# Layer norms of a second transformer block, with their sums made inside the product ahead of them

## The reference

```python
def _layer_norm(x, g, b, eps):
    mu = jnp.mean(xf, axis=-1, keepdims=True)
    var = jnp.mean(jnp.square(xf - mu), axis=-1, keepdims=True)
    return (xf - mu) * lax.rsqrt(var + eps) * g + b
...
for l in range(2):                       # ALPHA = 4 ** 0.25
    h = rwkv7_time_mix(x) if l == 0 else diff_attention(x, k_sh, v_sh)  # both end in @ w_o
    x = _layer_norm(ALPHA * x + h, ln_g[l, 0], ln_b[l, 0], 1e-5)
    x = _layer_norm(ALPHA * x + jnp.square(jax.nn.relu(x @ w1[l])) @ w2[l],
                    ln_g[l, 1], ln_b[l, 1], 1e-5)
```

## Time and profile before

| | us |
|---|---|
| median of 3 runs | 3045.97 (3044.67 to 3046.77) |
| the profiled execution's time | 3043.37 |
| its span | 3041.6 |
| PE busy | 2741.9 (90% of the span) |
| DVE, ACT, POOL busy | 1189.7, 517.5, 531.2 |
| mean granted TensorE clock | 0.928 of full speed |

### The profile page before, as it was taken

How to read it: one execution, slowest core, us unless ns; L and a number is a source line. 1 busy time by engine, 2 the same in 40 slices (tenths; PEclk the granted TensorE clock), 3 DMA queues, 4 the chain that set the end, 5 groups by cost and what they waited for, 6 DMA issues and landing times. The chain is left out here.

```text
span 3041.6 us, 45357 instructions
## 1 busy us (share of the span) xinstructions
PE 2741.9 (90%) x20202; PEld 2017.3 (66%) x20202; DVE 1189.7 (39%) x1791; ACT 517.5 (17%) x983; POOL 531.2 (17%) x304
## 2 busy tenths in 40 slices
PE   6999888977899997997888788999989998899997
PEld 4556577753688885443766646888854454688886
DVE  2221233443699944103565524442120062444312
ACT  3222112220211101013443301000010062100001
POOL 0000244520000000000222103344400000343331
PEclk9999867998899998998887888999989999899998
DMA  6222100020222123111000001222213100122220
GB/s 267 111 111 87 53 2 2 2 84 28 74 93 83 59 77 114 55 69 56 3 2 2 3 28 56 87 102 89 83 57 111 59 25 28 56 83 83 84 83 28
DMA packets 16210, 196.29 MB, mean 65 GB/s; under 512 B 1768, under 2 KB 1896, under 8 KB 4112
## 3 DMA queue, kind: packets, MB, share of 16 engines
q1 hardware_dynamic: 16016, 193.39, 16.8%
HBM read 191.27 MB, written 2.12 MB: 64 GB/s over the span
## 5 line engine op out<-in xcount | busy, mean ns | idle before, releaser
L2807 PE MATMUL psum<-arena,weight_ring 128*128 128x256 f32 x3072 | 674.6, 381 | 14.0 <-PEq L1607 14.0
L2807 PEld LDWEIGHTS psum<-arena,weight_ring 128*128 128x128 f32 x3072 | 587.7, 191 | 95.5 <-issue 14.5
L226 PE MATMUL psum<-arena,weight_ring 128*128 128x512 f32 x1024 | 450.7, 602 | 52.3 <-PEq L1474 26.1
L226 PEld LDWEIGHTS psum<-arena,weight_ring 128*128 128x128 f32 x1024 | 197.5, 194 | 302.2 <-issue 285.7
L1754 PE MATMUL psum<-arena,weight_ring 128*128 128x256 f32 x1584 | 349.3, 382 | 11.1 <-PEq L1607 7.0
L1754 PEld LDWEIGHTS psum<-arena,weight_ring 128*128 128x128 f32 x1584 | 303.5, 192 | 53.7 <-issue 11.7
L468 PE MATMUL psum<-arena,weight_ring 128*128 128x512 f32 (+1 forms) x672 | 248.2, 529 | 2.7 <-ACT arena L601 2.7
L2181 POOL TENSOR_TENSOR arena<-arena,consts_sb 128x512 f32<-128x512 f32 x48 | 64.5, 1350 | 1003.5 <-ACT arena L2473 775.4
L468 PEld LDWEIGHTS psum<-arena,weight_ring 128*128 128x128 f32 x672 | 128.2, 193 | 114.5 <-issue 106.4
L2855 POOL TENSOR_TENSOR arena<-weight_ring 128x1024 f32<-128x1024 f32 x32 | 77.0, 2407 | 548.5 <-issue 519.9
L2863 POOL TENSOR_TENSOR weight_ring<-arena,weight_ring 128x1024 f32<-128x1024 f32 x32 | 80.9, 2529 | 372.4 <-PE psum L2807 372.2
(11 more groups left out here) (410 smaller groups left out, 3397.9 us busy)
## 6 DMA issues: line engine op xcount, KB each, us to landing
weight_ring<-in_mlp_up SPq DMA_DIRECT2D x16, 2048.0 KB, 7.7
weight_ring<-in_mlp_down SPq DMA_DIRECT2D x16, 2048.0 KB, 7.7
weight_ring<-in_ada SPq DMA_DIRECT2D x12, 2048.0 KB, 13.0
weight_ring<-in_gate_up SPq DMA_DIRECT2D x11, 2048.0 KB, 7.6
weight_ring<-in_w_in SPq DMA_DIRECT2D x7, 2048.0 KB, 11.1
weight_ring<-in_w_o SPq DMA_DIRECT2D x4, 2048.0 KB, 7.8
weight_ring<-in_w_kv SPq DMA_DIRECT2D x4, 2048.0 KB, 8.0
weight_ring<-in_down_a SPq DMA_DIRECT2D x4, 1536.0 KB, 6.4
```

Source lines behind the costliest of these rows:

```text
L226: mm = pe.matmul(bank[:, 0:width], w[:, k, m * P:(m + 1) * P], rhs(k), start=(k == 0), stop=(k == kt - 1))
L2807: mm = pe.matmul(g.banks[i][:, pair * HALF:(pair + 1) * HALF], left[:, j, pair * P:(pair + 1) * P], right(j), start=first and j == 0, stop ...
```

## The change

The four `feature_norm` stages of the second block and `stage_store` are gone. Each norm's work is divided over the stage ahead of it and the stage behind it.

In the product ahead (`residual_product`, `mlp`): after the first output tile the token mean over that one tile's 128 features (a "shift") is made and subtracted from all tiles. Later tiles are scaled by ALPHA and shifted ahead of time, so that the eviction is a plain addition of the bank. VectorE keeps a running sum of the shifted tiles (`total`) and of their squares (`power`, the squares from ScalarE), and TensorE sums over the partitions only `total`, `power` and the last tile with its square. `tail_stats` then makes the mean, its square and that minus eps. In `mlp` the unit is not a tile but a part of 256 columns, 16 parts in four rounds; the TensorE work stands between products of chunks 10 and 15.

In the stage behind (`mlp`, `stage_qkv`, and a new `stage_last_norm`), the "head": variance, root, reciprocal, the two spreads, and then subtraction, multiplication and gain and bias tile by tile, each tile's `normed` counted. The stage's first products wait tile by tile: `mlp` does products 0, 2, 1, 3, ... of chunk 0 in that order, and makes each side as soon as its tiles are there; `stage_qkv` runs the first three key tiles in one loop over k. `stage_last_norm` writes each tile by a DMA of its own.

```diff
-def residual_product(g, chunks, kt, cols, src):
...
+def tile_sums(pe, g, bank, rows, quarters, first, last):
+    for i, j in enumerate(quarters):
+        mm = pe.matmul(bank[32 * j:32 * j + 32, 0:P], g.c.ones[:, 0:32], rows[:, i * P:(i + 1) * P],
+                       start=first, stop=last, skip_group_check=True)
+def tail_stats(g, dve, s):
+    dve.wait_ge(s.sums, 1)
+    dve.tensor_scalar(mean, g.banks[1][:, 0:P], 1.0 / D, None, ALU.mult).then_inc(s.stats, 1)
+    dve.wait_ge(s.stats, 1)
+    dve.tensor_tensor(square, mean, mean, ALU.mult).then_inc(s.stats, 1)
+    dve.wait_ge(s.stats, 2)
+    dve.tensor_scalar(square, square, -LN_EPS, None, ALU.add).then_inc(s.stats, 1)
...
+def residual_product(g, src):          # TensorE
+                    if m == 1:
+                        pe.wait_ge(g.acc_free, group0 + 1)
+                        tile_sums(pe, g, g.banks[7], x[:, 0, :], quarters, True, True).then_inc(s.first_sum, 1)
+                    if m == 2:
+                        pe.wait_ge(s.first_mean, 1)
+                        quarter_spread(pe, g, g.banks[5], first).then_inc(s.shift_all, 1)
+                pe.wait_ge(s.total, KD - 2)
+                tile_sums(pe, g, g.banks[1], total, quarters, True, False)
+                pe.wait_ge(s.power, KD - 2)
+                tile_sums(pe, g, g.banks[7], power, quarters, True, False)
+                tile_ready(pe, KD - 1)
+                tile_sums(pe, g, g.banks[1], x[:, KD - 1, :], quarters, False, True).then_inc(s.sums, 1)
+                pe.wait_ge(s.sq, KD)
+                tile_sums(pe, g, g.banks[7], sq[:, 1, :], quarters, False, True)
...
+def head_tiles(g, dve, s, lo, hi):
+    for k in range(lo, hi + 1):
+        if k == 0:
+            dve.wait_ge(s.mean_all, 1)
+        if k < hi or k == lo:
+            dve.tensor_tensor(x[:, k, :], x[:, k, :], g.banks[5][:, :], ALU.subtract).then_inc(s.centred, 1)
+        if k > lo:
+            dve.wait_ge(s.inv_all, 1)
+            dve.wait_ge(s.centred, k)
+            dve.tensor_tensor(x[:, k - 1, :], x[:, k - 1, :], g.banks[6][:, :], ALU.mult).then_inc(s.scaled, 1)
...
-def mlp(g):
+def mlp(g, norm):
+                            if c == 0 and pair == 0 and i < 2:
+                                pe.wait_ge(s.normed, 4 * i + j + 1)
...
+                def shift_work(c, i):
+                    if (c, i) == (UP + 2, 1):
+                        part_added(3)
+                        tile_sums(pe, g, g.banks[7], x[:, 0, :], range(4), True, True).then_inc(s.first_sum, 1)
+                    if (c, i) == (UP + 2, 4):
+                        pe.wait_ge(s.first_mean, 1)
+                        quarter_spread(pe, g, g.banks[7], first).then_inc(s.shift_all, 1)
+                    if (c, i) == (UP + 7, 5):
+                        pe.wait_ge(s.took, 6 * (UP + 3) + 1)
+                        pe.wait_ge(s.total, 10)
+                        pe.wait_ge(s.power, 10)
+                        for h in (0, 1):
+                            tile_sums(pe, g, g.banks[1], total[h], (2 * h, 2 * h + 1), True, False)
+                            tile_sums(pe, g, g.banks[7], power[h], (2 * h, 2 * h + 1), True, False)
+                        last_sums(12)
+                    if (c, i) == (UP + 7, 6):
+                        for n in (13, 14, 15):
+                            last_sums(n)
...
                     product(c, 0, a11, b11)
-                    product(c, 1, a12, b21)
+                    if c > 0:
+                        product(c, 1, a12, b21)
...
                     product(c, 2, s1, r1)
+                    if c == 0:
+                        product(c, 1, a12, b21)
...
+                first_product(UP + 5, UP + 2, HALF)          # ScalarE, down part
+                for n in range(4, 8):
+                    square(n)
+                first_product(UP + 7, UP + 3, HALF)
+                for n in range(8, 16):
+                    square(n)
...
+                head_inverse(g, dve, s)                      # VectorE, start of mlp
+                head_tiles(g, dve, s, 0, 5)
+                dve.wait_ge(s.normed, 4)
                 dve.tensor_tensor(up_t[0], x12, x11, ALU.subtract).then_inc(s.side, 1)
+                head_tiles(g, dve, s, 5, 8)
+                dve.wait_ge(s.normed, 8)
                 dve.tensor_tensor(up_t[2], x22, x12, ALU.subtract).then_inc(s.side, 1)
...
+                        if c < ALL - 1:                      # VectorE, after down_others of a round
+                            scale_and_shift((c - UP) // 2 + 1)
+                            add_up((c - UP) // 2)
...
-            sp.dma_start(g.out, x[:, :, :]).then_inc(g.stored, 16)
+                for k in range(KD):
+                    sp.wait_ge(s.normed, k + 1)
+                    sp.dma_start(g.out[:, k, :], x[:, k, :]).then_inc(g.stored, 16)
```

More of the change, by code:

```diff
@@ L2728, in _ @@
                 dve.wait_ge(s.out, KD)
[L2731 to L2743 removed]
+NORM_STAT_AT, SQUARE_AT, SHIFT_AT, FIRST_AT, TOTAL_AT = 12288, 12800, 13824, 14336, 14464
@@ new lines, with head_pe, head_act @@
+HEAD_SEMS = ("var", "root", "inv", "mean_all", "inv_all", "centred", "scaled", "normed")
+def head_pe(g, pe, s):
+    mean, _, inv = norm_stats(g)
+    quarter_spread(pe, g, g.banks[5], mean).then_inc(s.mean_all, 1)
+    pe.wait_ge(s.inv, 1)
+    quarter_spread(pe, g, g.banks[6], inv).then_inc(s.inv_all, 1)
+def head_act(g, act, s, n):
+    x, inv = view(g, X_AT, KD, SEQ), norm_stats(g)[2]
+    act.wait_ge(s.var, 1)
+    act.activation(inv, inv, ACT.Sqrt).then_inc(s.root, 1)
+    for k in range(KD):
+        act.wait_ge(s.scaled, k + 1)
+        act.activation(x[:, k, :], x[:, k, :], ACT.Identity, bias=g.v.ln_b[:, 8 * n + k:8 * n + k + 1],
+                       scale=g.v.ln_g[:, 8 * n + k:8 * n + k + 1]).then_inc(s.normed, 1)
@@ L2768, in mlp @@
     UP, ALL = 8, 16
+    sq = [view(g, at + HALF, HALF) for at in (MLP_V_AT, 35328 - HALF)] + [g.c.lvl[:, SEQ:SEQ + HALF], view(g, MLP_S1_AT, HALF)]
+    first = view(g, 35584, P)
+    shift = [view(g, at + HALF, HALF) for at in (MLP_P1_AT, MLP_U2_AT)]
+    parts = [(t, h) for m in range(4) for t, h in ((m, 0), (m + 4, 1), (m + 4, 0), (m, 1))]
+    down0 = group0 + KF2
+    total, power = ([at[:, HALF * h:HALF * h + HALF] for h in (0, 1)] for at in (g.c.lvl, g.c.scan))
     def quads(c):
@@ L2785, in mlp, with part_ready, part @@
     with ExitStack() as ctx:
-        s = stage_sems(g, ctx, "sums", "side", "side4", "prod", "p1", "took", "hid", "added")
+        s = stage_sems(g, ctx, "w_sums", "side", "side4", "prod", "p1", "took", "hid", "order", "added", "first_sum", "first_mean",
+                       "shift_all", "shift", "shifted", "sq", "total", "power", "sums", "stats", *HEAD_SEMS)
+        def part_ready(eng, n):
+            if n < 4:
+                eng.wait_ge(s.shifted, n + 1)
+            elif n % 4 == 3:
+                eng.wait_ge(g.acc_free, down0 + 2 * (n // 4) + 2)
+            else:
+                eng.wait_ge(s.added, 3 * (n // 4) + n % 4 + 1)
+        def part(n):
+            t, h = parts[n]
+            return x[:, t, HALF * h:HALF * h + HALF]
         with nc.Block() as block:
@@ L2801, in product @@
                             pe.wait_ge(g.acc_free, free_groups(r))
+                        elif i == 5 and r > UP:
+                            pe.wait_ge(s.added, 3 * (r - UP))
                         else:
@@ new lines, in down_others, with take_shift @@
+                    dve.tensor_tensor(x[:, m, hi], x[:, m, hi], g.banks[6][:, lo], ALU.add).then_inc(g.acc_free, 2)
+                def take_shift():
+                    dve.wait_ge(s.first_sum, 1)
+                    dve.tensor_scalar(first, g.banks[7][:, 0:P], 1.0 / P, None, ALU.mult).then_inc(s.first_mean, 1)
+                    dve.wait_ge(s.shift, 2)
+                    dve.wait_ge(s.added, 3)
+                    dve.wait_ge(g.acc_free, down0 + 2)
+                    for n in range(4):
+                        dve.tensor_tensor(part(n), part(n), shift[parts[n][1]], ALU.subtract).then_inc(s.shifted, 1)
```

274 lines of the change are left out of this document (221 added, 53 removed).

## The result

The changed kernel takes 2995.36 us (median of 4 runs, 2991.83 to 2999.48), the kernel before 3045.66 (4 runs). The ratio is 0.9835, 95% interval 0.9818 to 0.9852: 50 us less, where 47.6 were forecast (2998, range 2989 to 3008). The profiled execution took 2991.83, its span is 2990.0, the granted clock 0.939 on the mean.

The account below looks back on a forecast made before the run. TensorE is busy nine tenths of the span, so only its latency holes at the four norms can give: 23.8 + 13.6 + 10.2 = 47.6 off 3043.4 makes 2995.8, plus 2.6 for a median, rounded to 2998, range 2989 to 3008.

Parts of the forecast that it names:

- The chain of the head: Norm 0, counted from T, the last product's end: head at T + 2.65, product 0 at T + 7.1, tile 3 ready at 10.65.
- Norms 0 and 2: Norm and chunk 0 end at T + 36.7 instead of 49.7, less 1.1 in the product ahead: 11.9 us each.
- the hole: TensorE's gap at norm 0, from the last product of one stage to the first of the next: 22.4 us.
- the clock: Chunk 0 behind norms 0 and 2: the low TensorE clock was taken to cost 3.1 us.
- Norm 1: Norm and four key tiles end at T + 36.0 instead of 51.7, less 2.1 in `mlp`: 13.6 us saved.
- Norm 3: Last norm to the end: 16.8 instead of 29.1, less 2.1 for the down part: 10.2 us saved.
- A: Heads: the low clock lasts longer, a second 6 us stretch costing each of three heads 3: 3007; chance 0.12.
- worst form: All of chunk 0 and the first keys run at 1.2 GHz, 67 us more: 3065; chance 0.02.
- B: Last round of `mlp`: VectorE is late with its sums, TensorE stands 4 to 6 us in each: 3008; chance 0.08.
- C: Heads: the tile-by-tile start fails, the first product runs only once the eighth tile is normed: 3020; chance 0.03.
- D: Heads: the clock does not fall at all behind T, the last product's end: 2990.5; chance 0.05.

Follow-up runs that it names:

- no_shift: Changed kernel with the shift left out, evictions scaling and adding as before the change: 2991.76 us, ratio 0.9822.
- no_shift_fill: Changed kernel without the shift and with six matmuls of constants in the head of `mlp`: 2987.98 us, ratio 0.9807.
- fill: Changed kernel with six matmuls of constants put into the head of `mlp`: 2994.29 us, ratio 0.9826.
- all_normed: Changed kernel with the first product of each `mlp` and the first key matmul waiting for all eight tiles: 3017.76 us, ratio 0.9915.
- subs_first: Changed kernel with all eight subtractions of the head ahead of all multiplications: 3008.88 us, ratio 0.9878.
- busy60: Changed kernel with 60 extra VectorE operations in round 2's sums of each `mlp`'s down part: 3018.18 us (one run).
- fill_keys: Changed kernel with six matmuls of constants in the head of `mlp` and three ahead of the first key matmul: 2994.46 us, ratio 0.9839.

## Why the prediction was right

**The chain of the head.** Every step fell within 0.2 us of its forecast up to the fourth matmul: head at T + 2.65 (2.66 measured), first matmul at 7.1 (7.2), fourth at 10.65 (10.7). The durations came from the same operations in the earlier trace rows, and the alternation's pitch of 1.22 is in the rows (1.20). The four terms that I gave for the head's start add up to 2.56, not 2.65; that the stated figure met the measured one is luck of 0.1. Luck too is that the second spread ran at full clock: I had read from the earlier trace rows that the clock falls 8.1 us behind T, and it fell at about T + 10 in this kernel, but at T + 4.5 in no_shift and no_shift_fill, where the same spread took 1.94 and 1.97 instead of 1.16.

**Norms 0 and 2.** Forecast 13.0 less for the hole and chunk 0, and 1.1 more in the product; measured 14.7 and 14.6 less, 1.45 and 1.5 more. The term that was mis-sized is the clock: I let the fourth matmul, product 0's second half and a stretch after it run at 1.2 GHz, 3.1 us in all, and took chunk 0 to T + 36.7. It ended at about T + 35.1, with the clock low for some 3.5 us. fill, whose clock does not fall in the head, ends it 1.25 sooner, so the term was 1.25 and not 3.1.

**Norm 1.** Forecast 15.7 less at the keys, 2.1 more in each `mlp`; measured 17.0 and 2.7. The 1.7 for the clock were not paid at all: it stayed at 1.00 through the keys. all_normed shows the other side: there the clock was low from T + 5 until the late keys had run for 5.5 us, and the same stretch lost 3.7 to it. Inside `mlp` I had counted the matmuls' bare durations for the shift; no_shift shows that its sum and spread cost 1.45 where I had 1.1. The other 1.2 are the sums ahead of product 6, where I had 1.0.

**Norm 3.** Forecast 12.3 less to the end, measured 11.4. The store of 256 KB lands 2.0 behind its issue, and the kernel ends 2.9 behind it, where I had 2.2 for all. The Trainium skill, "DMA: Bandwidth & Descriptors", section "Anatomy of one DMA", gives a fit for another issue path, from which my estimate was 2.6; the measured landing of 2.0 is below that, the distance to the kernel's end of 2.9 above it.

**The sum.** From the w_o product on 49.4, forecast 47.6. The errors have both signs: norms 0 and 2 gained 3.3 and the keys 1.3 more than forecast, mostly because I had charged too much for the clock; the insertions into the w_o products cost 0.8 more and those into `mlp` 1.1 more, and the end took 0.9 longer. So 4.6 one way stand against 2.8 the other, and that only 1.8 is left is in part luck. The median came out 3.0 below the forecast: 1.8 of that are these, and the other 1.2 are less than the stages ahead vary by between executions.

**Rivals.** A, a longer low clock, did not come about in the changed kernel, where the clock is low for less than forecast. In its neighbours it does: 1.5 at the keys in fill, 1.2 at each head and 1.7 at the keys in no_shift, 2.6 at the keys in subs_first. Its worst form never came near. B: VectorE made round 2's sums by 2213.1, 10.2 us ahead of TensorE; busy60 measures that margin. The slowing beside GpSimd appears as forecast (the additions to `power` take 0.41 alone and up to 2.57, 1.27 on the mean), and is hidden. C: each of the first matmuls does wait for its own tile, and all_normed shows what C would have cost. D came about at the keys alone; fill brings it about in the two `mlp` heads, 1.25 each.

## What to carry to other kernels

Where the engine that bounds a kernel stands still for a reduction, split the reduction: keep running sums beside the product that makes its input, and let the consumer start on the first tile of the result. Count for each consumer which tile it needs first, since only that one's time is paid, besides the clock (the first for the keys, the fourth for `mlp`). Compare traces by stretches between fixed instructions: in the second block of this program they repeated to 0.05 us in the one kernel that was profiled twice, while the runs of one kernel scatter by 2 to 16. Then check the sum of the stretches against the medians, as all_normed shows.

## What the runs showed of the hardware that was not expected

- The start of the w_o product, behind stages that no kernel here alters, lies anywhere between 1767.8 and 1779.6 in 12 profiled executions. In the two of the changed kernel the second block repeats to hundredths, and what varies ahead of it is the clock: the same 1126 matmul records took 58.0 us at 0.86 in one and 61.5 at 0.79 in the other.
- Whether TensorE's clock falls at a given gap differs between kernels whose edits lie hundreds of us away: the same key instructions took 34.74 with the clock at 1.00 and 36.2 to 36.5 with some 3.4 us at 0.50. So an edit that saves 1 us elsewhere can be masked by a loss of 1.5. The gaps need not be long: in no_shift the clock fell at T + 4.5, when TensorE had been idle for no more than 0.83 us at a time, between groups of small matmuls. Six constant matmuls in the gaps kept the clock at 1.00 through both `mlp` heads in fill and fill_keys; in the two kernels without the shift it fell ahead of them and was back 3.4 us later. What sets the fall stays open, and with one profiled execution per edited kernel, so does how much of it is the edit's and how much the execution's.
